# Conditioning in full blocks of 2048 columns, a quarter in each strip of the array, and level scores in column strips

## The reference

```python
c_act = jax.nn.silu(c)
mod = (c_act @ p['w_ada'][l] + p['b_ada'][l])[:, None, :]
sh1, sc1, g1, sh2, sc2, g2 = split_cols(mod, [D_MODEL] * 6)
h = rms_norm(x, p['norm_mix'][l]) * (1.0 + sc1) + sh1
...
x = x + g1 * y
h = rms_norm(x, p['norm_mlp'][l]) * (1.0 + sc2) + sh2
x = x + g2 * sq_relu_mlp(h, p['mlp_w_up'][l], p['mlp_w_down'][l])
```

```python
scores = jnp.einsum('bhtd,bhtsd,bhsd->bhts', qc, decay, kc)
o_intra = jnp.einsum('bhts,bhse->bhte', scores, vc)
```

## Time and profile before

| | |
|---|---|
| median of 3 runs | 2621.56 us (2620.45 to 2622.38) |
| profiled execution, its own time | 2624.08 us |
| its span | 2622.1 us |
| TensorE busy | 2569.0 us, 98% |
| VectorE busy | 1543.8 us, 59% |
| ScalarE busy | 980.4 us, 37% |
| mean granted clock of TensorE | 0.991 |
| moved by DMA | 616.30 MB, mean 235 GB/s |

### The profile page before, as it was taken

How to read it: one execution, slowest core, us unless ns; L and a number is a source line. 1 busy time by engine, 2 the same in 40 slices (tenths; PEclk the granted TensorE clock), 3 DMA queues, 4 the chain that set the end, 5 groups by cost and what they waited for, 6 DMA issues and landing times.

```text
span 2622.1 us, 51350 instructions
## 1 busy us (share of the span) xinstructions
PE 2569.0 (98%) x20965; PEld 2389.5 (91%) x20965; DVE 1543.8 (59%) x2338; ACT 980.4 (37%) x1105; POOL 142.9 (5%) x188
## 2 busy tenths in 40 slices
PE   7899999999999999999999999999999999999998
PEld 4589788889989889899999999989999999999998
DVE  3475445555455445545557987987664555555654
ACT  2133243323323323233335555455433333333333
POOL 1000151100000000000020010100000000000011
PEclk8899999999999999999999999999999999999999
DMA  9998979799988899899655454554555555655553
GB/s 357 348 296 266 298 256 325 253 324 309 309 296 306 300 305 306 300 303 307 222 180 172 145 174 155 172 178 157 166 183 178 177 176 179 179 181 180 179 176 129
DMA packets 504966, 616.30 MB, mean 235 GB/s; under 512 B 10535, under 2 KB 412293, under 8 KB 504553
## 3 DMA queue, kind: packets, MB, share of 16 engines
q1 hardware_dynamic: 498130, 591.70, 68.7%
q0 software_dynamic: 6720, 22.96, 2.7%
HBM read 602.77 MB, written 13.26 MB: 235 GB/s over the span
## 4 chain that ended last, share of the span: by engine, by line
PE 89%; DVE 4%; DMA 4%; ACT 2%; issue 1%; SPq 0%; POOL 0%; ACTq 0%; DVEq 0%; POOLq 0%
PE ps L891 25%; PE ps L892 25%; PE ps L893 25%; PE pm L1008 5%; DMA wide<-in_w_ada 2%; PE pm L1170 1%; PE ps L932 1%; PE pm L1022 1%; DVE w_lo L2044 1%; PE pm L988 1%; ACT w_hi L1520 1%; PE pm L1249 0%; DVE z L2621 0%; PE ps L1081 0%; DVE acc L2621 0%
## 5 line engine op out<-in xcount | busy, mean ns | idle before, releaser
L2044 DVE TENSOR_TENSOR w_lo<-raw,w_hi 128x1024 fp32r<-128x1024 f32 x708 | 878.0, 1242 | 860.4 <-ACT w_hi L1520 854.6
L1520 ACT ACTIVATE w_hi<-raw 128x1024 fp32r<-128x1024 f32 x696 | 736.3, 1059 | 1261.4 <-PE ps L893 1242.6
L891 PE MATMUL ps<-h_hi,w_hi 128*128 128x264 f32 x3616 | 1048.2, 290 | 6.5 <-DVE h_lo L2469 3.0
L892 PE MATMUL ps<-h_lo,w_hi 128*128 128x264 f32 x3616 | 1030.5, 285 | 0.0
L893 PE MATMUL ps<-h_hi,w_lo 128*128 128x264 f32 x3616 | 1029.3, 285 | 0.0
L891 PEld LDWEIGHTS ps<-h_hi,w_hi 128*128 128x128 f32 x3616 | 683.7, 189 | 36.2 <-issue 28.6
L892 PEld LDWEIGHTS ps<-h_lo,w_hi 128*128 128x128 f32 x3616 | 682.6, 189 | 0.8
L893 PEld LDWEIGHTS ps<-h_hi,w_lo 128*128 128x128 f32 x3616 | 682.2, 189 | 0.0
L891 PE MATMUL ps<-f_hi,w_hi 128*128 128x264 f32 x2048 | 585.1, 286 | 0.0
L892 PE MATMUL ps<-f_lo,w_hi 128*128 128x264 f32 x2048 | 583.8, 285 | 0.0
L893 PE MATMUL ps<-f_hi,w_lo 128*128 128x264 f32 x2048 | 582.9, 285 | 0.0
(11 more groups left out here) (374 smaller groups left out, 1724.9 us busy)
## 6 DMA issues: line engine op xcount, KB each, us to landing
raw<-in_mlp_w_up SPq DMA_DIRECT2D x128, 1024.0 KB, 6.4
raw<-in_mlp_w_down SPq DMA_DIRECT2D x128, 1024.0 KB, 5.4
wide<-in_w_ada SPq DMA_DIRECT2D x104, 1024.0 KB, 9.1
wide_late<-in_w_ada SPq DMA_DIRECT2D x56, 1024.0 KB, 9.5
raw<-in_od_w_in SPq DMA_DIRECT2D x48, 1024.0 KB, 5.2
raw<-in_ev_w_in SPq DMA_DIRECT2D x32, 1024.0 KB, 6.5
araw<-in_w_ada SPq DMA_DIRECT2D x24, 1024.0 KB, 9.9
raw<-in_ev_w_out SPq DMA_DIRECT2D x16, 1024.0 KB, 5.9
```

Source lines behind the costliest of these rows:

```text
L891: nc.tensor.matmul(acc, w_hi[:, slot, cols], xh[:, k, :], start=(k == UK * ends[0]), stop=False)
L892: nc.tensor.matmul(acc, w_hi[:, slot, cols], xl[:, k, :], start=False, stop=False)
L1520: nc.scalar.activation(w_hi[:, u, :], raw[:, p, u, :], ACT.Copy).then_inc(hi_ready, 1)
L2044: nc.vector.tensor_tensor(w_lo[:, p, u, :], raw[:, p, u, :], w_hi[:, u, :].bitcast(F32), ALU.subtract).then_inc(lo_ready, 1)
```

## The change

A late block now has 2048 columns: strip q takes the columns 512 q to 512 q + 511 of it, and all 16 row tiles k one after another. A transfer brings one row tile (128 rows of 2048 columns, runs of 8 KB), 1 MB as before. The four pairs of a phase of `gemm` each do four row tiles (`full_part`, 16 products of 512 columns), and only behind the last pair's part come one copy, four transposes and one addition of the bias (`full_add`, `add_rates`); nothing has to be summed. In input projection 0 the 16 steps beside the groups do two row tiles each, eight steps make a block (g1, then sc2). The prologue's blocks stay as they are. The level scores are made strip by strip: for each left strip of 32 keys one product with only those right-half queries that belong to its blocks. TensorE's loop over the pairs is written out where a late block runs beside it.

```diff
-ADA_IN0, ADA_OUT0, ADA_MLP0, ADA_ALL = 0, 16, 24, 80
-ADA_PAIRED = 8
...
+PAIR_STEPS = 8
+ADA_STEPS = 2 * PAIR_STEPS
+ADA_RATES = (G1, SC2)
...
+        def left_strips(lv):
...
+            w = 1 << lv
+            return range(CH // CP) if w < CP else [s for s in range(CH // CP) if s * CP % (2 * w) < w]
+
+        def right_of_strip(t, lv, s):
...
+            w = 1 << lv
+            if w < CP:
+                return t[:, s * CP:(s + 1) * CP].rearrange("p (n s w) -> p n s w", s=2, w=w)[:, :, 1, :]
+            begin = s * CP // (2 * w) * 2 * w + w
+            return t[:, begin:begin + w]
...
-                sp.dma_start((wides if isinstance(w, int) and w < WIDE_MLP0 else wides_late)[c][:, :, :], view[:, 4 * c:4 * c + 4, bass.ds(col, WIDE)]).then_inc(wide_in[c], 16)
...
+                sp.dma_start((wides if isinstance(w, int) and w < PART_MLP0 else wides_late)[c][:, :, :], rate_row(view, k0 + c, col)
+                             ).then_inc(wide_in[c], 16)
...
-                        if w is not None and u == 1 + late:
-                            wide_half(w, 0, chunks)
-                            wide_half(w, 1, chunks)
-                        if w is not None and u == 2 + late:
-                            wide_turn(w)
+                        if j is not None and u == 1 + late:
+                            full_part(*full, j, chunks)
+                        if j == QUARTERS - 1 and u == 2:
+                            wide_turn(full[0])
...
-                with pe.Fori(1 if first else 0, count // 2 - (norm is not None)) as j:
-                    one(2 * j, 0)
-                    one(2 * j + 1, 1, None if w0 is None else w0 + j)
+                if full is None:
...
+                else:
+                    for j in range(1 if first else 0, pairs - (norm is not None)):
+                        one(2 * j, 0)
+                        one(2 * j + 1, 1, j)
...
-                    for r in range(2):
-                        for q in range(4):
-                            k = 8 * h + 4 * r + q
-                            last = nc.tensor.matmul(acc3[q * CP:(q + 1) * CP, :], c_pad[:, k, :], buf[:, 4 * r + q, :],
-                                                    start=(k < 4), stop=(k >= KT - 4), tile_position=(0, q * CP))
+                    k = 2 * (a % PAIR_STEPS) + h
+                    for q in range(QUARTERS):
+                        last = nc.tensor.matmul(pm[q * CP:(q + 1) * CP, 3, :], c_pad[:, k, :], buf[:, q, :],
+                                                start=(k == 0), stop=(k == KT - 1), tile_position=(0, q * CP))
                     last.then_inc(ada_used, 1)
...
+            def full_part(b, w, j, chunks):
...
+                if j == 0:
+                    pe.wait_ge(wide_rows, b)
+                for c in range(4):
+                    pe.wait_ge(wide_in[c], 16 * (w + (j + 1)))
+                    k = 4 * j + c
+                    for q in range(QUARTERS):
+                        last = nc.tensor.matmul(pm[q * CP:(q + 1) * CP, 3, :], c_pad[:, k, :], chunks[c][:, q, :],
+                                                start=(k == 0), stop=(k == KT - 1), tile_position=(0, q * CP))
+                    last.then_inc(wide_used, 1)
...
-                            else:
-                                last = nc.tensor.matmul(right_half(dst[:, h, :], i - 1), lhs[c][h], right_half(rhs[c][h], i - 1),
-                                                        start=True, stop=True)
+                                continue
+                            for s in left_strips(i - 1):
+                                own_rows = dst[s * CP:(s + 1) * CP, h, :]
+                                last = nc.tensor.matmul(right_of_strip(own_rows, i - 1, s), lhs[c][h][:, s * CP:(s + 1) * CP],
+                                                        right_of_strip(rhs[c][h], i - 1, s), start=True, stop=True,
+                                                        tile_position=(0, s * CP))
...
+            def add_rates(bank, c):
...
+            def full_add(b, c):
...
+                dve.wait_ge(wide_turned, b + 1)
+                add_rates(2, c).then_inc(wide_ready, 1)
+                dve.wait_ge(wide_ready, b + 1)
```

More of the change, by code:

```diff
@@ L963, in earlier_squares @@
                         sums(sqa[:, :, :], True, False)
+                pairs = count // 2
                 if first:
                     first_group(g, first)
-                    one(1, 1, w0, late=1)
-                with pe.Fori(1 if first else 0, count // 2 - (norm is not None)) as j:
-                    one(2 * j, 0)
-                    one(2 * j + 1, 1, None if w0 is None else w0 + j)
+                    one(1, 1, None if full is None else 0, late=1)
+                if full is None:
+                    with pe.Fori(1 if first else 0, pairs - (norm is not None)) as j:
+                        one(2 * j, 0)
+                        one(2 * j + 1, 1)
+                else:
+                    for j in range(1 if first else 0, pairs - (norm is not None)):
+                        one(2 * j, 0)
+                        one(2 * j + 1, 1, j)
                 if norm is None:
@@ L973, in gemm @@
                 one(count - 2, 0)
-                one(count - 1, 1, None if w0 is None else w0 + (count // 2 - 1), earlier_squares)
+                one(count - 1, 1, None if full is None else pairs - 1, earlier_squares)
             def ada_group(a):
-                if isinstance(a, int) and a == 0:
+                if a == 0:
                     pe.wait_ge(wide_rows, WIDES)
-                else:
-                    pe.wait_ge(mod_ready, a)
+                elif a == PAIR_STEPS:
+                    pe.wait_ge(mod_ready, 1)
                 for h in range(2):
@@ L2054, in pass_over, with lo_phase, body @@
                 nc.vector.memset(skipped[:, 1:2], 0.0).then_inc(lo_ready, NU)
-            def lo_phase(count, n, evac, last_next=None, w0=None, tile0=None, ends=False, begun=None):
-                def body(i, p, nxt, b=None, seam=False, late=0):
+            def lo_phase(count, n, evac, last_next=None, full=None, tile0=None, ends=False, begun=None):
+                def body(i, p, nxt, seam=False, last=False):
                     for u in range(NU):
@@ L2063, in body @@
                             lo(nxt, u, 1 - p)
-                        if w0 is not None and b is not None and u == 1 + late:
-                            wide_copy(w0 + b)
-                        if w0 is not None and b is not None and u == 2 + late:
-                            wide_add(w0 + b, tile0 + QUARTERS * b)
+                        if full and last and u == 1:
+                            wide_copy(full[0], full[1] + (QUARTERS - 1))
+                        if full and last and u == 2:
+                            full_add(full[0], tile0)
                     evac(i, p, n + i)
@@ L2084, in lo_phase, with ada_rows @@
                     return
[L2085 to L2090 removed]
+                body(count - 1, 1, last_next, ends, last=True)
+            def ada_rows(b):
+                dve.wait_ge(ada_used, 2 * PAIR_STEPS * (b + 1))
+                if b == 0:
                     dve.wait_ge(wide_turned, WIDES)
                 else:
[L2093 to L2094 removed]
```

206 lines of the change are left out of this document (94 added, 112 removed).

## The result

The changed kernel took 2595.8 us (median of 4 runs, 2592.2 to 2599.9), the kernel before 2622.0 us on the same chip: 0.9895 of it, 95% interval 0.9883 to 0.9908. In a second measurement, later, it was 2597.0 against 2623.7 us, 0.9902 (0.9885 to 0.9918). The prediction was 2594.5 us. So the total is right within 3 us. The experiments show that three of its terms were not, and that the total came out right by luck: their errors cancel in part, and about 4 us of the gain stay unexplained.

What follows compares the result with a forecast made beforehand. TensorE, busy 98% of the span, was taken as the bound. 10.6 + 2.6 + 0.5 + 1.0 + 12.4 = 27.1 us off gave 2594.5 us for the median; likeliest range 2587 to 2600 (0.55), wider range 2584 to 2611.

Steps and rivals of the forecast that it cites:

- Late transposes: Late conditioning blocks: 32 sets of four transposes become 8, 24 sets fewer at 0.44 us each, -10.6 us.
- Input projection 0: Layer 0 input projection: fewer transposes -2.6 us, wider conditioning products -0.5; VectorE's conditioning work before the first level gone, -1.0.
- 14.7: All conditioning terms together: 10.6 + 2.6 + 0.5 + 1.0 = 14.7 us less.
- Levels: Level scores in strips, seven levels in each of three recurrences: -12.4 us after cuts for transfers and VectorE.
- The wave of four strips: Level scores: four 16-column passes, one in each strip, priced at 0.045 us; issue bound 0.036, loads 0.027.
- 5.35: Level scores: us saved per recurrence by TensorE alone; 4.6 expected in layer 0, 2.5 in the first layer 1 recurrence.
- The rivals on the price: Level scores: short passes cost 0.029 us each, 2609 us (chance 0.18); or from 0.040, at 0.058 2643 us (chance 0.08).
- The 0.32 us for going into the strips and out of them: Level scores: both changes of TensorE's tiling mode cost 0.32 us together, counted 21 times in the sum.
- Code: Layer 0 MLP and output projection: inner loops written out on TensorE, 8,369 to 11,479 listed rows, price 0.
- the cover that the prediction named: Straight-line input projection, fetched with DMA engines at 0.97, keeps TensorE busy 60.50 of 60.50 us; hence price 0.
- a loop's edge costs nothing: Main products beside conditioning blocks in layer 0 MLP: each takes its ordinary 0.122 us step, so loop edges cost nothing.
- code arrives late: Rival, layer 0 MLP: each of 28 pairs of groups loses 0.5 us to a fetch, +14, 2608 us; chance 0.07.

Runs made afterwards that it cites:

- experiment 7: The changed kernel with TensorE's loop over the middle chunks written out and the first set of scores in strips too: 2587.2 us (0.9861).
- experiment 2, second kernel: The kernel before with TensorE's pair loops in output projection 0 and layer 0 MLP, and its loop over the middle chunks, written out: 2624.7 us (1.0004).
- experiment 2: The kernel before with TensorE's pair loops written out: 2630.5 us (1.0024); with its loop over the middle chunks written out as well: 2624.7 us (1.0004).

## Why the prediction was right, and where it was wrong

**Late transposes, forecast -10.6.** Right: 27.65 - 27.23 = 0.42 us instead of 0.44 for a set of four, 10.1 for 24. The conditioning's products kept their 3.57 us.

**Input projection 0, forecast -2.6, -0.5 and -1.0.** Right in mechanism. From the first set of scores to the first level there are now 9.88 us (155.66 to 165.54), 11.55 before; the forecast's terms for this stretch are 1.0 and one pair of transposes, 1.2. What the conditioning saves does not all come through: with the jump taken out it gave 10.9 us alone, not 14.7, and its trace loses 3.8 us of its lead behind recurrence 0's levels.

**Levels, forecast -12.4.** Wrong in two sizes, and both made the gain too small. The wave of four strips was taken as 0.045 us, between issue and load; 64 passes take 0.55 us, 0.034 a wave, the issue bound that the prediction had as 0.036 and did not take. Levels of 16 columns save 0.93 us instead of 0.75; levels 5 and 6 (0.96 and 0.58 saved) were right within 0.03. A recurrence saves 6.2 us by TensorE, not 5.35. The second size is how much comes through: 5.35 was cut to 4.6 in recurrence 0 and to 2.5 in recurrence 1, since the transfers and VectorE were nearly full. That step failed. VectorE was busy 47.28 of 48 us and TensorE 47.58, so a busy share of 92% in the stretch before was not the most that VectorE can reach. With one set of scores cheaper still, in experiment 7, the limit was reached. The strips alone gave 17.1 us. The place where the neighbours do take something back is the one behind the levels, at the states of recurrence 0, and the prediction did not look there.

**The rivals on the price** fell: 0.0087 us a pass, not 0.029; in the four strips nearly all passes start 0 to 17 ns behind the one before. The Trainium skill's page "TensorEngine Tiling (Array Packing)", section Instruction Overhead, gives some 60 cycles for every product. The runs differ: 32 products, 64 passes, start within 0.55 us, 0.017 us a product or 41 cycles at 2.4 GHz; the measurement decides. The 0.32 us for going into the strips and out of them fit the rows of all three forms of level as forecast.

**Code, forecast 0.** Wrong, and the cover that the prediction named was the wrong one to ask about. Straight-line code did cost nothing that can be told from noise (experiment 2, second kernel: +1 us, within its interval), and so did each pair. What it missed is the loop around the written-out pairs: its body, written out, no longer stays, and the jump back stops TensorE for 4 us and halves its clock for 3: 5.5 to 5.9 us in the traces of the changed kernel, 5.5 by the medians of experiment 2. The prediction's sentence that a loop's edge costs nothing was read at an edge whose code stays. The rival "code arrives late" had the right resource, a wrong place (28 pairs instead of one jump) and, by that, 14 us instead of 5.5.

**The sum.** From the experiments: conditioning 10.9, strips 17.1, the jump -5.5, makes 22.5 us, against 26.1 and 26.6 measured. The other 4 us are open. A place where they can lie is the stretch between recurrence 0's levels and output projection 0, since its two waits can be shared: the strips alone lose 4.2 us of their lead there, the conditioning with the jump taken out 3.8, and both parts together only 1.5 to 2.0 in four traces. But this is not shown. The same conditioning lost 1.6 us there with the jump, which comes later, and gained 2.6 in the kernel with the 96 waits; in these three traces the lead at output projection 0 was 2.5 to 3.4 us, whether it had been 0.8, 4.7 or 6.3. The prediction's 27.1 had 3.8 too much for the conditioning, 4.7 too little for the levels, and no jump. That 2594.5 was so close is luck.

## What to carry to other kernels

When a loop's body is written out, look at the loop around it: count the code of the whole body against what the fetches show to stay, and write the outer loop out too where it runs only twice; longer straight code was free here, a jump back in long code cost 5 to 10 us in the traces. Where only blocks of a score matrix are used, make them strip by strip: 64 short passes in four strips cost half of 16 full ones, as long as a level doesn't use up a packet of code. And a neighbour engine's high busy share does not say that it will hold a gain back, nor that it will not: look for the next wait that stands on a chain of its own, here the round trip of the states through the DMA engines.

## What the runs showed of the hardware that was not expected

- The second pass of a loop of long code fetches all of it again (19 packets of 16 KB in 280 us), where the shorter body before needed none.
- The gap at the jump was 3.2 to 4.5 us from product to product, and a second one of 3.7 us came or went with 96 waits ahead of it that do nothing. The products went on 2.3 to 2.8 us after a packet of code had started. The profile named three different releasers for the first gap: VectorE's residual update, its low part of the weights, and "issue".
- After the gaps at the jump TensorE's granted clock fell close to its lower level. Behind the 4 us gap it did so at once, for 3.0 us; behind the shorter one (2.94 us idle) the first ten products came every 0.12 us, and then 15 every 0.22. Behind a wait of 1.8 us for VectorE it fell too, for 3.2 us.
- 128 passes of 16 columns and their loads in 1.24 us outrun the supply of code at five of 15 levels: four gaps of 1.3 to 1.7 us and one of 0.6.
